# Moving the sums of weight quarters from VectorE to GpSimd in a seven-product FFN

## The reference, cut to what matters

```
h = rmsnorm(x, g_ffn_pre)
f = (jax.nn.silu(h @ w_ffn_gate) * (h @ w_ffn_up)) @ w_ffn_down
x = x + rmsnorm(f, g_ffn_post)
```

## Time and profile before

| | |
|---|---|
| median of 3 runs | 1001.41 us (1001.06 to 1001.5) |
| profiled execution, its time | 1001.08 us |
| profiled execution, its span | 999.2 us |
| TensorE busy | 978.2 us (98%) |
| VectorE busy | 632.1 us (63%) |
| ScalarE busy | 397.0 us (40%) |
| GpSimd busy | 85.7 us (9%) |
| granted TensorE clock | 0.996 of full speed |

### The profile page before, as it was taken

The page is one execution under the profiler, slowest core; times in us unless marked ns, Lnnn a source line. Parts: engine busy times, 40 slices in busy tenths (PEclk is TensorE's granted clock), DMA queues, the critical chain, the costliest instruction groups (busy, mean ns, idle before and its releaser), DMA issues.

```text
span 999.2 us, 19155 instructions
## 1 busy us (share of the span) xinstructions
PE 978.2 (98%) x7256; PEld 954.8 (96%) x7256; DVE 632.1 (63%) x1244; ACT 397.0 (40%) x693; POOL 85.7 (9%) x140
## 2 busy tenths in 40 slices
PE   6999999999999999999998999999999999999997
PEld 5999999999999999999998999999999999999997
DVE  5555666757665634345466899625996469965762
ACT  5324434434343422223454555424453135533252
POOL 1032212212100000010011100000000000030000
PEclk9999999999999999999999999999999999999999
DMA  8434222122222222246512623521334223274211
GB/s 210 126 111 131 82 69 58 58 73 64 62 65 64 84 86 76 82 131 193 151 31 59 228 78 92 148 64 45 110 95 133 64 72 98 81 249 136 85 47 50
DMA packets 166198, 98.45 MB, mean 99 GB/s; under 512 B 14657, under 2 KB 162529, under 8 KB 165873
## 3 DMA queue, kind: packets, MB, share of 16 engines
q1 hardware_dynamic: 159904, 79.19, 28.0%
q0 software_dynamic: 4336, 16.67, 4.7%
q10 hardware_dynamic: 1888, 1.64, 0.6%
HBM read 86.79 MB, written 10.75 MB: 98 GB/s over the span
## 4 chain that ended last, share of the span: by engine, by line
PE 91%; DVE 4%; issue 2%; ACT 2%; DMA 0%; DVEq 0%; SPq 0%; ACTq 0%
PE acc L679 35%; PE acc L942 10%; PE acc L943 10%; PE acc L944 10%; PE small L942 6%; PE small L943 6%; PE small L944 6%; PE small L811 1%; PE small L828 1%; PE small L857 1%; PE small L861 1%; PE small L759 1%; PE small L859 1%; PE small L1095 1%; ACT prob L1183 1%
## 5 line engine op out<-in xcount | busy, mean ns | idle before, releaser
L679 PE MATMUL acc<-xh,whi 128*128 128x288 f32 x736 | 163.1, 303 | 1.6 <-DVE wlo L1606 1.5
L679 PE MATMUL acc<-xh,wlo 128*128 128x288 f32 x736 | 157.3, 295 | 0.0
L679 PE MATMUL acc<-xl,whi 128*128 128x288 f32 x736 | 157.2, 295 | 0.0
L1123 ACT ACTIVATE whi<-raw 128x1024 fp32r<-128x1024 f32 (+1 forms) x62 | 62.1, 1001 | 198.3 <-PE acc L679 198.3
L1606 DVE TENSOR_TENSOR wlo<-raw,whi 128x1024 fp32r<-128x1024 f32 (+1 forms) x64 | 74.2, 1160 | 81.1 <-ACT whi L1123 77.7
L679 PEld LDWEIGHTS acc<-xh,whi 128*128 128x128 f32 x736 | 116.9, 189 | 6.1 <-issue 5.0
L679 PEld LDWEIGHTS acc<-xl,whi 128*128 128x128 f32 x736 | 118.1, 188 | 0.0
L679 PEld LDWEIGHTS acc<-xh,wlo 128*128 128x128 f32 x736 | 118.0, 188 | 0.0
L1918 DVE TENSOR_TENSOR wlo<-raw,whi 128x512 fp32r<-128x512 f32 (+2 forms) x93 | 80.9, 871 | 51.1 <-ACT whi L1334 35.4
L942 PE MATMUL acc<-yh,whi 128*128 128x288 f32 x360 | 107.3, 298 | 1.3 <-DVE wlo L1918 1.3
L944 PE MATMUL acc<-yh,wlo 128*128 128x288 f32 x360 | 106.1, 295 | 0.0
(11 more groups left out here) (312 smaller groups left out, 2353.8 us busy)
## 6 DMA issues: line engine op xcount, KB each, us to landing
raw<-in_w_in SPq DMA_DIRECT2D x92, 256.0 KB, 3.1
raw<-in_w_ffn_gate SPq DMA_DIRECT2D x44, 256.0 KB, 3.3
raw<-in_w_ffn_up SPq DMA_DIRECT2D x44, 256.0 KB, 4.0
raw<-in_w_ffn_down SPq DMA_DIRECT2D x32, 256.0 KB, 3.5
res<-x_scratch POOLq DMA_DIRECT2D x16, 288.0 KB, 3.8
raw<-in_w_branch_ret SPq DMA_DIRECT2D x16, 256.0 KB, 3.1
raw<-in_w_out SPq DMA_DIRECT2D x16, 256.0 KB, 4.0
raw<-in_w_ffn_down SPq DMA_DIRECT2D x16, 192.0 KB, 3.7
```

Of the source, the lines that this page charges most:

```text
L679: ins = nc.tensor.matmul(acc[:, a, hf, 0:HALF], w[:, s, at:at + P], x(k)[:, hf * HALF:(hf + 1) * HALF], start=first and n == 0 and m == 0, ...
L1123: nc.scalar.activation(whi[:, s, 0:n], raw[:, s, 0:n], ACT.Copy).then_inc(hi_ready, 1)
```

## The change

The four sums of a pair leave VectorE's program and are made by GpSimd, in the same four places of `s_sum`. VectorE keeps the low parts, ScalarE the high parts, and both wait on the same semaphores as before. GpSimd makes the sums of all 19 pairs in one straight loop behind the issue of the residual's DMAs (L2425). A sum of pair i waits for both loads of pair i, and from the second pair on also for the low part of the same product of pair i - 1, which is the last reader of that place.

```diff
-            def sum_of(i, t):
-
-
-                a, b = (("prod", i, n) for n in range(2))
-                for part in (a, b):
-                    dve.wait_ge(loaded[RAW[part]], LOADS[part])
-                a0, a1 = raw_of(RAW[a])[:, 0:QUART], raw_of(RAW[a])[:, QUART:2 * QUART]
-                b0, b1 = raw_of(RAW[b])[:, 0:QUART], raw_of(RAW[b])[:, QUART:2 * QUART]
-                s1, s2 = s_sum[:, S_STEP[PS1], :], s_sum[:, S_STEP[PS2], :]
-                first, second = {PS1: (b0, b1), PS2: (s1, a0), PS4: (s2, a1), PS3: (a0, b0)}[t]
-                if t in (PS2, PS4):
-                    dve.wait_ge(s_ready, 4 * (i - PLAIN) + S_STEP[t])
-                nc.vector.tensor_tensor(s_sum[:, S_STEP[t], :], first, second, ALU.add).then_inc(s_ready, 1)
-
             def product_operand(i, t):
 
-                if t == PA0:
-                    sum_of(i, PS1)
-                elif t == PS1:
-                    sum_of(i, PS2)
-                elif t == PS2:
-                    sum_of(i, PS4)
-                elif t == PA1:
-                    sum_of(i, PS3)
                 lo(("prod", i, t))
...
+            def sum_of(i, t):
+
+
+                a, b = (("prod", i, n) for n in range(2))
+                if i > PLAIN:
+                    pool.wait_ge(lo_ready, MADE[("prod", i - 1, t)])
+                for part in (a, b):
+                    pool.wait_ge(loaded[RAW[part]], LOADS[part])
...
+                if t in (PS2, PS4):
+                    pool.wait_ge(s_ready, 4 * (i - PLAIN) + S_STEP[t])
+                nc.gpsimd.tensor_tensor(s_sum[:, S_STEP[t], :], first, second, ALU.add).then_inc(s_ready, 1)
+
+            for i in range(PLAIN, FT):
+                for t in (PS1, PS2, PS4, PS3):
+                    sum_of(i, t)
             pool.wait_ge(res_parked, 32)
```

More of the change, by code:

```diff
@@ L2426, in _ @@
                                res[:, half, :]).then_inc(res_parked, 16)
+            def sum_of(i, t):
[4 more added lines that the diff above has]
+                    pool.wait_ge(loaded[RAW[part]], LOADS[part])
+                a0, a1 = raw_of(RAW[a])[:, 0:QUART], raw_of(RAW[a])[:, QUART:2 * QUART]
+                b0, b1 = raw_of(RAW[b])[:, 0:QUART], raw_of(RAW[b])[:, QUART:2 * QUART]
+                s1, s2 = s_sum[:, S_STEP[PS1], :], s_sum[:, S_STEP[PS2], :]
+                first, second = {PS1: (b0, b1), PS2: (s1, a0), PS4: (s2, a1), PS3: (a0, b0)}[t]
+                if t in (PS2, PS4):
[4 more added lines that the diff above has]
+                    sum_of(i, t)
             pool.wait_ge(res_parked, 32)
```

## The result

The change makes the kernel slower: 1004.99 us median (1003.22 to 1006.31, 9 runs) against 1001.09 (1000.44 to 1002.18, 9 runs), a ratio of 1.0033 (95% interval 1.0024 to 1.0042). That is 3.3 us by the ratio and 3.9 by the medians, where the forecast sum was 1.4. A second set of runs of the same kernel gave 1004.07 (1003.01 to 1005.46, 5 runs) beside 1000.81 of the kernel before, a ratio of 1.0040 (1.0026 to 1.0053). The profiled execution took 1005.53 us, with a span of 1003.3.

The account below looks back on a forecast made before the run. TensorE bounds the kernel, busy 978.2 of 999.2 us, with VectorE only just fast enough. Waits of 0.6 ahead of the pairs, 0.8 in the first group and 0 later add 1.4 to 1001.08: 1002.5 us, range 1001.0 to 1008.0.

Parts of the forecast that it names:

- what is removed is worth 0: Taking 76 sums off VectorE, 46 us in all, gains nothing on TensorE's path, since TensorE never waits there.
- who stands in whose way: GpSimd's SBUF sums hold VectorE's low parts back by up to 1.1 us each; reads of PSUM go on.
- VectorE's pair: One pair takes VectorE 9.3 + 2.6 = 11.9 us, against 10.9 before and 11.1 on TensorE.
- ahead of the pairs: GpSimd's first four sums delay VectorE 3.6 us; unit 4's low part ends at 566.0 and TensorE waits 0.6 us.
- second and third group: These groups start without arrears; VectorE needs 74.2 us of 78, so TensorE loses 0.
- VectorE saves six sums up to pair 3's results (3.6 us) and is held by pair 4's four sums (4.4): 0.8 later.: First group's start: VectorE's net lateness is 0.8 us, before 2.9 more from pairs 3, 4 and 5.
- 3.7 is within the margin of 4.5: First group: VectorE's 3.7 us of lateness stays under the 4.5 us in hand at PA0's low part.
- `f_low`: End of the first group: last low part comes 2.5 us later with a margin of 1.7, so TensorE waits 0.8 us.
- A: Rival: nothing blocks or sums find gaps, no margin is touched; 1001.0 to 1001.6 us; chance 0.25 shared with C.
- B: Rival: VectorE becomes the bound, from 2.9 us of holding per pair; 1008 at 3.5, about 1020 at 4.4; chance 0.32.
- C: Rival: GpSimd's sums come too late and ScalarE waits for them; 1001.4 us; chance 0.25 shared with A.
- D: Rival: the kernel gets faster, needing a TensorE wait on this work that no row shows; chance 0.05.

Follow-up runs that it names:

- The add and the fill on a tile of its own: Kernel before, VectorE keeping its sums, plus 76 GpSimd adds or fills on a tile nobody else uses: 1015.32 us with adds, 1000.57 us with fills.
- pair 3 alone: Changed kernel, but GpSimd makes only the four sums of pair 3, VectorE all others: 999.84 us, ratio 0.9997 to the kernel before.
- the kernel of the first group: Changed kernel, but GpSimd makes only the sums of pairs 3 to 7, VectorE the rest: 1003.37 us, ratio 1.0034 to the kernel before.
- The late start of GpSimd's sums: Changed kernel, with GpSimd's first four sums waiting until FFN unit 5's low part is made: 1002.56 us, ratio 1.0023 to the kernel before.
- pairs 4 to 21: Changed kernel, but VectorE makes pair 3's four sums and GpSimd all others: 1003.45 us, ratio 1.0031 to the kernel before.
- groups two and three: Changed kernel, but GpSimd makes only the sums of pairs 8 to 21, VectorE those of pairs 3 to 7: 1000.90 us, ratio 1.0005.
- pair 4: Changed kernel, but GpSimd makes only pair 4's four sums, VectorE all others: 1000.90 us, ratio 1.0002 to the kernel before.
- pairs 4 and 5: Changed kernel, but GpSimd makes only the sums of pairs 4 and 5, VectorE all others: 1001.26 us, ratio 1.0003 to the kernel before.

## Why the prediction was off by 2 us

**Right: what is removed is worth 0.** No sums at all gives no gain.

**Right: who stands in whose way.** 1.1 us of holding for one instruction, PSUM reads go on, and GpSimd's add is 1.28 us. The add and the fill on a tile of its own show that the reading does it. (The row of 1.28 us that the prediction leaned on is an instruction with one tile to read; that those with two are held is seen first in the changed kernel, by the low part of 1.78.)

**Right: VectorE's pair.** `u_sums` start at 591.37, 603.78, 614.95 and 626.62: 12.41, 11.17 and 11.67, a mean of 11.75 (12.07 in the second set), where 11.9 was forecast and 10.91 was before. One such pair, VectorE's timeline; 1.36 and the first of the two low parts are held, PSUM reads are not (GpSimd's sums behind them):

```profile
609.60 0.45 DVE L2146 TENSOR_TENSOR up<-small,kept 128x288 f32<-128x288 f32 x1
610.08 1.36 DVE L2150 SCALAR_TENSOR_TENSOR ta<-up,tb 128x576 f32<-128x576 f32 x1
611.37 2.39 DVE L1918 TENSOR_TENSOR wlo<-raw,whi 128x512 fp32r<-128x512 f32 x2
613.68 0.74 DVE L2112 TENSOR_TENSOR fl<-ta,fh 128x576 fp32r<-128x576 f32 x1
614.35 0.68 DVE L1918 TENSOR_TENSOR wlo<-s_sum,whi 128x512 fp32r<-128x512 f32 x1
614.95 0.44 DVE L2121 TENSOR_TENSOR kept<-acc,kept 128x288 f32<-128x288 f32 x1
...
609.30 1.53 POOL L2419 TENSOR_TENSOR s_sum<-s_sum,raw 128x512 f32<-128x512 f32 x1 [0.17 <-POOL s_sum L2419]
610.79 1.82 POOL L2419 TENSOR_TENSOR s_sum<-raw 128x512 f32<-128x512 f32 x1
```

**Right: ahead of the pairs.** The low part of unit 4 was forecast to end at 566.0 and ended at 564.07 + 2.31 = 566.38. TensorE lost 0.69 us there, for a forecast of 0.6. The size is in part luck. The same four sums cost 0.96 us in the second set, 0.8 with pair 3 alone, 0.69 here and nothing in the kernel of the first group, in the order of the granted clock from 551 to 556 us: 0.79, 0.72, 0.66 and 0.53. The slower TensorE came to unit 4, the less it waited there.

**Right: second and third group.** 0, as forecast.

**Wrong: "VectorE saves six sums up to pair 3's results (3.6 us) and is held by pair 4's four sums (4.4): 0.8 later."** The 3.6 us of holding ahead of the pairs had been worked out one line above, and priced only at unit 4's low part. The sum let the first group start without it. VectorE does stand idle there, but only to wait for ScalarE, which itself waits for VectorE's `ta` (571.15 before, 575.14 after), so the idle time moves along and makes nothing good. The first low part of pair 3 starts at 578.25 in place of 574.26, 3.5 late less the offset. The wait for ScalarE in front of it has even grown from 1.57 to 2.17 us: the first of the six saved sums saved nothing. So `u_sums` of pair 3 was 3.6 us late, not 0.8. On the way the low part of pair 3's last product was later still. It ended at 587.72 + 1.78 = 589.50, where it had ended at 584.18, and TensorE, which came to it at 587.66 before and so had 3.5 us in hand, lost 0.84 us. That wait was in no part of the sum. The late start of GpSimd's sums takes both away (late at pair 3: 2.2 us). Here is the stretch, VectorE after:

```profile
585.36 2.44 DVE L2063 TENSOR_TENSOR tl<-t_high_part,th 128x1152 fp32r<-128x1152 f32 x1
587.72 1.78 DVE L1918 TENSOR_TENSOR wlo<-raw,whi 128x512 fp32r<-128x512 f32 x1
...
591.37 0.45 DVE L2121 TENSOR_TENSOR kept<-acc,kept 128x288 f32<-128x288 f32 x1
```

**Wrong: "3.7 is within the margin of 4.5."** The margin was taken at an operand, the low part of PA0. A nearer one is the PSUM bank of PS1: TensorE may start PS1 of the next pair when `u_sums` of this one has read its second bank. Behind the last of the earlier trace rows, VectorE in the kernel before:

```profile
620.49 0.46 DVE L2145 TENSOR_TENSOR kept<-acc,kept 128x288 f32<-128x288 f32 x1
```

It is free at 620.95, and TensorE's next PS1 starts at 624.28: 3.3 us. Two pairs earlier it is 599.1 and 602.00: 2.9. The table above shows the step: no wait at 1.8 us of lateness, one at 3.5. In the changed kernel the second read ends at 604.26 + 0.46 = 604.72, and PS1 starts at 604.86.

**Near by luck: `f_low`.** 0.56 us lost, for 0.8 forecast. But VectorE's last `f_low` ended 5.1 us late (642.54 + 0.75 = 643.29 for 637.73, less the offset), not 2.5, and TensorE, by then 3.0 us behind itself, came that much later for it. Two errors nearly cancel.

**The sum, mended.** 0.69 at unit 4, 0.84 at pair 3's last product, 0.86 at the bank, 0.43 at pair 5's last product, 0.56 at `f_low`, and 0.2 of small steps: 3.6 us, for 1.4. Of the 2.2 missing, 2.1 is the three waits that were not in it.

**The rivals.** A fell (low parts are held). B's mechanism, VectorE as the bound, is what happened, but in the first group alone, and through a margin and arrears that its price did not have, not through a b above 2.9 (b is the holding in one pair; a pair of 11.75 us is 9.3 + 2.45). Nothing was seen of C: no matmul waited for a sum. D's door is shut by the kernel without sums.

**No better version came out.** The split of the work that costs nothing (GpSimd's sums in the second and third group alone) is as fast as the kernel before and no faster.

## What to carry to other kernels

When a fully loaded engine is delayed, carry the delay through every later consumer until an idle gap eats it; a wait that was priced once is not paid off. Look for the smallest margin among all that the engine releases, PSUM banks as well as operands, since the first to run out sets the cost. And before work is moved off a busy engine, ask what TensorE waits for now: here the answer was nothing, and even leaving the work out altogether gained nothing.

## What the runs showed of the hardware

**GpSimd's fills pass freely, its reads do not.** 76 fills of 128x512 (527 ns each) changed neither VectorE's low parts (median 684 ns, maximum 693) nor the time. The Trainium skill's page "SBUF — State Buffer" (section "SBUF: two separate sides") counts a VectorE instruction with two SBUF inputs as a party to the lock only against a GpSimd instruction that reads SBUF; the trace agrees, by the 693 ns beside the fills and the 1531 ns beside the adds.

**A wait costs TensorE more than its length.** Five waits of 2.16 us in all cost 3.4 us of drift, 0.16 to 0.27 each beyond the bracket. The row that ends a wait is also longer (0.37 to 0.40 us in place of 0.29).

**The same wait is followed by a lower clock in one execution and not in another.** Ahead of the last norm TensorE waits 1.50 us for a sum of squares, in the kernel before as in the changed one. After it the granted clock was 0.52 for 3 us in the kernel before, half of the full 2.4 GHz, and 15 matmuls ran. By stretch:

```profile
923.00:926.00 3.00, 3.00 (x15) 3.00 (x15) 1.03 (x3) 0.44 (x1) 0.87 (x1) 0.52 0.20 58
```

In the second set's profiled execution of the changed kernel, after the same wait, it stayed full, and 25 ran:

```profile
926.50:929.50 3.00, 3.00 (x25) 3.00 (x26) 1.64 (x5) 0.44 (x1) 0.88 (x1) 1.00 0.29 82
```

By matching the matmuls on both sides of this place, full clock there is worth 1.5 us. Of the profiled executions, those of the kernel before, the changed kernel's first, pairs 4 to 21, groups two and three, and the one without sums had the lower clock. Seven others with the same wait had not (the changed kernel again, its late start, the first group, pair 3, pair 4, pairs 4 and 5, the fills), nor had the one with adds, after 2.12 us. What decides it is open. It is why the drift was used for the account. Whether it also explains why medians stand up to 1.8 us off the drift is not shown, since only profiled executions tell their clock there. The largest case is pair 3 alone: 0.8 us of drift, and a median 1.0 below the kernel before (its ratio, 0.9997, is 0.3 us below).
